# State-space turns written out with tables built ahead, a folded Fourier part, and late modulation columns on TensorE

## The reference

```
mod = c @ w_ada + b_ada                     # 6 vectors of 1024: sh_m, sc_m, gt_m, sh_f, sc_f, gt_f
h = rms_norm(x, g_pre_mix) * (1 + sc_m) + sh_m
u, f, q, k, v = split(h @ w_in)             # widths 384, 256, 384, 128, 128
y_ssm = s5_mixer(u, ...)                    # 24 groups of 16 channels, 64 complex states, both directions
y_fft = real(fft2(f over positions and over the 64 channels of a head)) @ w_fft
y_att = window_attention(q, k, v, sink)
x = x + gt_m * rms_norm(concat(y_ssm, y_fft, y_att) @ w_out, g_post_mix)
```

## Time and profile before

| | us |
|---|---|
| median of 3 runs | 3899.11 |
| lowest and highest | 3894.24, 3900.86 |
| the profiled execution | 3903.71 |
| its span, first to last instruction | 3901.9 |

### The profile page before, as it was taken

How to read it: one execution, slowest core, us unless ns; L and a number is a source line. 1 busy time by engine, 2 the same in 40 slices (tenths; PEclk the granted TensorE clock), 3 DMA queues, 4 the chain that set the end, 5 groups by cost and what they waited for, 6 DMA issues and landing times.

```text
span 3901.9 us, 41628 instructions
## 1 busy us (share of the span) xinstructions
PE 3400.1 (87%) x15935; PEld 2817.1 (72%) x15935; DVE 1191.4 (31%) x1793; ACT 790.4 (20%) x1395; POOL 1551.0 (40%) x1271
## 2 busy tenths in 40 slices
PE   6773334798999999999999999987788999999977
PEld 4663333687888878888888888876666888888866
DVE  4744664525233323210001123135534100001323
ACT  3020002513111112210000113136533100001222
POOL 3137663052333356523233573210025233336743
PEclk8887666999999999999999999989999999999999
DMA  4551001143111124311112333534433111122432
GB/s 170 152 181 44 7 7 38 45 157 130 44 54 43 54 103 140 97 54 43 54 43 82 118 118 122 166 116 107 108 108 108 44 54 43 54 81 99 149 108 92
DMA packets 261359, 344.97 MB, mean 88 GB/s; under 512 B 24726, under 2 KB 203209, under 8 KB 261234
## 3 DMA queue, kind: packets, MB, share of 16 engines
q1 hardware_dynamic: 217784, 258.76, 22.0%
q10 hardware_dynamic: 43098, 84.05, 5.9%
q0 software_dynamic: 352, 0.44, 0.0%
HBM read 293.50 MB, written 56.00 MB: 90 GB/s over the span
## 4 chain that ended last, share of the span: by engine, by line
PE 75%; DVE 11%; ACT 5%; issue 4%; DMA 2%; POOL 2%; SPq 0%; DVEq 0%; ACTq 0%; POOLq 0%
PE PS L811 67%; PE PS L1856 3%; DVE ot L1592 1%; PE PS L747 1%; DVE pl_ab L1964 1%; DVE pt L680 1%; PE PS L1544 1%; DMA w_raw<-w_up 1%; DVE oo L1593 1%; PE PS L1532 1%; ACT ph_ab L1901 1%; ACT act L702 1%; DVE t L1608 1%; ACT pr_ab L1891 1%; POOL w_lo L251 1%
## 5 line engine op out<-in xcount | busy, mean ns | idle before, releaser
L251 POOL TENSOR_TENSOR w_lo<-w_raw,w_hi 128x512 fp32r<-128x512 f32 x724 | 970.2, 1371 | 155.5 <-ACT w_hi L1303 130.9
L247 POOL CAST w_hi<-w_raw 128x2048 fp32r<-128x2048 f32 x173 | 335.7, 1941 | 1608.2 <-DMA w_raw<-ffn_w_gu 607.2
L811 PE MATMUL PS<-h_hi,w_hi 128*128 128x512 f32 x2482 | 803.6, 395 | 19.3 <-DVE h_lo L805 12.0
L811 PE MATMUL PS<-h_lo,w_hi 128*128 128x512 f32 x2482 | 796.6, 392 | 0.0
L811 PE MATMUL PS<-h_hi,w_lo 128*128 128x512 f32 x2482 | 796.0, 391 | 0.0
L811 PEld LDWEIGHTS PS<-h_hi,w_hi 128*128 128x128 f32 x2482 | 469.7, 189 | 120.0 <-DVE h_lo L805 16.6
L811 PEld LDWEIGHTS PS<-h_hi,w_lo 128*128 128x128 f32 x2482 | 469.8, 189 | 98.8
L811 PEld LDWEIGHTS PS<-h_lo,w_hi 128*128 128x128 f32 x2482 | 470.4, 190 | 95.7
L811 PE MATMUL PS<-w_hi,a_hi 128*128 128x512 f32 x1056 | 327.8, 392 | 9.5 <-DVE a_lo L877 7.2
L811 PE MATMUL PS<-w_lo,a_hi 128*128 128x512 f32 x1056 | 327.5, 392 | 0.0
L811 PE MATMUL PS<-w_hi,a_lo 128*128 128x512 f32 x1056 | 327.4, 391 | 0.0
...
## 6 DMA issues: line engine op xcount, KB each, us to landing
w_raw<-ffn_w_gu SPq DMA_DIRECT2D x88, 512.0 KB, 4.6
w_raw<-ffn_w_down SPq DMA_DIRECT2D x88, 512.0 KB, 4.2
w_raw<-w_up SPq DMA_DIRECT2D x44, 512.0 KB, 5.0
w_raw<-w_down SPq DMA_DIRECT2D x44, 512.0 KB, 4.2
xs<-px ACTq DMA_DIRECT2D x40, 512.0 KB, 2.6
w_raw<-w_out SPq DMA_DIRECT2D x32, 512.0 KB, 4.5
w_raw<-w_in SPq DMA_DIRECT2D x28, 512.0 KB, 5.1
...
```

Source lines behind the costliest of these rows:

```text
L247: e.tensor_copy(w_hi[b][:, 0:n], w_raw[b][:, 0:n]).then_inc(S("w_hi"), 1)
L251: op = e.tensor_tensor(w_lo[b][:, s], w_raw[b][:, s], w_hi[b][:, s].bitcast(F32), ALU.subtract)
L811: mm = e.matmul(o, a[ai], b[bi], start=start and first, stop=stop and end)
```

## The change

- `chain_dve` is cut in two: the exponential part (`chain_exp_dve`) runs in the start, ahead of the first modulation sums. The powers 2 to 8 are made by doubling, in 18 wider operations instead of 42. The exp on ScalarE and the head matrices of the Fourier part move to the start too.
- The four late modulation vectors leave VectorE and SP. GpSimd loads their 32 pieces into four buffers during the turns, and TensorE multiplies each with a column of c and adds all up in one PSUM bank. One sequence of gates follows behind the turns. The m slots go.
- u goes to DRAM from ScalarE and comes back in the order that the turns need, in 8 loads of SP. The t slots go.
- Fourier: since cosine is even and sine odd, f is folded (`fold_dve`) to 512 positions, the DFT table is 512 x 512 twice in 2 chunks, and output positions 513 to 1023 come from sums and differences (`fft_out_dve`). Position 512 is added by one-row matmuls with alternating signs. GpSimd makes both halves of the two chunks.
- Turns: written out one by one. All tables are made by VectorE. The rotations of all turns are cut into 16 x 8 factors (`rotations_dve`: copies and seven groups of four small operations), and `ssm_cs` multiplies them out per turn. `oo` has two buffers and is made one turn ahead, as is `gs_`. The sum `d_skip * u` becomes a 16 x 16 diagonal matmul. Outputs are formed channels first, so that GELU is done per turn, and go through DRAM (`yd`) into `yT`, instead of y_nat and the transposes.
- w_glu stage: VectorE multiplies with each sigmoid as soon as it is there.

The diff, cut to its core:

```diff
         G_Z1 = seg("z1", "cols", cols(t["w_in"]), 5)
-        G_DFT = seg("dft", "rows", rows(t["dft"]), 8)
+        G_DFT = seg("dft", "rows", rows(t["dft"]), 2)
...
-        def late_sp(e, first, end):
-            for i in range(first, end):
-                if i < 2:
-                    e.wait_ge(S("ht_lo"), 16)
-                else:
-                    e.wait_ge(S("lacc"), i - 1)
-                v, k = 2 + i // 8, i % 8
-                e.dma_start(lw[i % 2][:], t["w_ada"][0][k * P:(k + 1) * P, v * D:(v + 1) * D]).then_inc(S(f"lw_ld{i % 2}"), 16)
...
+        def ada_late_pe(e, first, end):
+            for q in range(first, end):
+                v, k = q // KT, q % KT
+                e.wait_ge(S(f"adl_ld{q % 4}"), 16 * (q // 4 + 1))
+                for h in range(2):
+                    r = 2 * v + h
+                    mm = e.matmul(PS[0:8, 0, :], cz[:, k, 7 - r:15 - r], adl[q % 4][:, h * 512:(h + 1) * 512],
+                                  start=q == 0 and h == 0, stop=q == 31 and h == 1)
+                mm.then_inc(S("ad_mm"), 1)
+        def ada_late_pool(e):
+            e.wait_ge(S("ff_y2"), 3)
+            for q in range(32):
+                v, k = q // KT + 2, q % KT
+                wait(e, S("ad_mm"), q - 3)
+                e.dma_start(adl[q % 4][:], t["w_ada"][0][k * P:(k + 1) * P, v * D:(v + 1) * D]).then_inc(S(f"adl_ld{q % 4}"), 16)
...
+            pr, pi = pw[:, PR:PR + CH + 1, :], pw[:, PI:PI + CH + 1, :]
+            for w in (1, 2, 4):
+                lo, hi = slice(1, w + 1), slice(w + 1, 2 * w + 1)
+                rw, iw = (v[:, w:w + 1, :].to_broadcast([2 * G, w, P]) for v in (pr, pi))
+                u, v = pwt[:, 0, 0:w, :], pwt[:, 1, 0:w, :]
+                tt(u, pr[:, lo, :], rw, ALU.mult)
+                tt(v, pi[:, lo, :], iw, ALU.mult)
+                tt(pr[:, hi, :], u, v, ALU.subtract)
+                tt(u, pr[:, lo, :], iw, ALU.mult)
+                tt(v, pi[:, lo, :], rw, ALU.mult)
+                tt(pi[:, hi, :], u, v, ALU.add)
+            e.wait_ge(S("sk_ld"), 32)
+            e.tensor_scalar(nsk[:], sk[:], -1.0, None, ALU.mult).then_inc(S("nsk"), 1)
             e.memset(junk[:, 0:1], 0.0).then_inc(S("pw"), 1)
...
         Z1 = [(0, "u", 0, P, 0, 0, 0), (0, "u", P, P, 0, 0, 1), (1, "u", 0, P, 0, 0, 2), (1, "f", P, P, 0, 0, 0),
-              (2, "f", 0, P, 0, 0, 1), (2, "q", P, P, 0, 0, 0), (3, "q", 0, P, 0, 0, 1), (3, "m", 0, P, 0, 0, 2),
-              (3, "q", P, P, 0, 0, 2), (4, "p", 0, P, 0, 0, 0), (4, "k", 0, P, 0, 0, 3), (4, "m", 0, P, 0, 0, 3),
-              (4, "p", 0, P, 0, 0, 1), (4, "t", 0, P, 0, 8, 0), (4, "t", 0, P, 0, 8, 1), (4, "v", P, P, 0, 8, 0),
-              (4, "t", 0, P, 0, 8, 2), (4, "m", 0, P, 0, 0, 4)]
-        u_tr = at("u_tr", [P, 3, SEQ], F32, 16 * KB)
+              (2, "f", 0, P, 0, 0, 1), (2, "q", P, P, 0, 0, 0), (3, "q", 0, P, 0, 0, 1), (4, "p", 0, P, 0, 0, 0),
+              (3, "q", P, P, 0, 0, 2), (4, "p", 0, P, 0, 0, 1), (4, "k", 0, P, 0, 0, 3), (4, "v", P, P, 0, 8, 0)]
+        u_tr = at("u_tr", [P, 3, CH, NCH], F32, 16 * KB)
...
+        def fold_dve(e):
+            e.memset(fm[:, :, 0:1], 0.0).then_inc(S("ff_fold"), 1)
+            e.wait_ge(S("z_uf"), 5)
+            e.tensor_tensor(fm[:, :, 1:512], fT[:, :, 1:512], fT[:, :, 1023:512:-1], ALU.subtract).then_inc(S("ff_fold"), 1)
+            e.tensor_tensor(fT[:, :, 1:512], fT[:, :, 1:512], fT[:, :, 1023:512:-1], ALU.add).then_inc(S("ff_fold"), 1)
...
-                    e.wait_ge(S("ff_lo"), T - 3)
-                for a in range(2):
-                    mm = e.matmul(PS[:, 4 + T % 4, a * 256:(a + 1) * 256], fT[:, a, T * P:(T + 1) * P],
-                                  bd[:, a, :, :].rearrange("p c n -> p (c n)"), start=True, stop=True)
-                mm.then_inc(S("ff_p"), 1)
-            e.wait_ge(S("ff_lo"), TT)
-            for kt in range(TT):
-                g = G_DFT + kt
+                mm = e.matmul(PS[0:1, 0, a * P:(a + 1) * P], fT[:, a, 512:513], bd[:, a, 0, :], start=True, stop=True)
+            mm.then_inc(S("ff_p"), 1)
+            e.wait_ge(S("ff_lo"), 5)
+            e.wait_ge(S("ff_hi"), 7)
+            for a in range(2):
+                cs = slice(a * P, (a + 1) * P)
+                for T in range(4):
+                    for q in (fp_hi, fp_lo):
+                        e.matmul(PS[:, 4, 2 * a:2 * a + 2], q[:, T, a, 0:P], altc[:], start=T == 0 and q is fp_hi, stop=False)
+                e.matmul(PS[:, 4, 2 * a:2 * a + 2], row_hi[:, cs], altr[:, 0:2], start=False, stop=False)
...
+        def fft_out_dve(e):
+            e.wait_ge(S("ff_os"), 1)
+            e.wait_ge(S("w_used"), G_DFT + 2)
+            e.tensor_tensor(yf[:, :, 0:512], PS[:, 0:2, :], os_[:], ALU.add).then_inc(S("ff_yf"), 1)
+            e.tensor_tensor(yf[:, :, 513:SEQ], PS[:, 0:2, 511:0:-1], os_[:, :, 511:0:-1], ALU.subtract).then_inc(S("ff_yf"), 1)
+            e.wait_ge(S("ff_y"), 1)
+            e.tensor_tensor(hl0[:, 3:5, :], yf[:, :, 0:512], hh[0][:, 3:5, :].bitcast(F32), ALU.subtract).then_inc(S("ff_y2"), 1)
...
+        def rotations_dve(e):
+            ta = own(e)
+            e.wait_ge(S("pw_ev"), 2)
...
+        def ssm_oo(e, ta, i):
...
+            g0 = i * GSUB
...
+            o = oo[i % 2]
+            for d in range(2):
+                qr, qi = (PR, PI) if d == 0 else (PRD, PID)
+                r, m = (st4(q, 9, d, g0).rearrange("p t g -> p g t").unsqueeze(3).to_broadcast([P, GSUB, 9, GC]) for q in (qr, qi))
+                c = [cc[:, k].rearrange("p (g c) -> p g c", c=GC)[:, g0:g0 + GSUB].unsqueeze(2).to_broadcast([P, GSUB, 9, GC])
+                     for k in range(2)]
+                for k in range(2):
+                    ta.add(e.tensor_tensor(o[:, k, d], r, c[k], ALU.mult))
+                if d:
+                    e.wait_ge(S("ss_oo"), 4 * i + 2)
+                for k in range(2):
+                    ta.add(e.tensor_tensor(oy[:, k], m, c[1 - k], ALU.mult))
+                ta.settle()
+                e.tensor_tensor(o[:, 0, d], o[:, 0, d], oy[:, 0], ALU.add).then_inc(S("ss_oo"), 1)
...
+        def ssm_cs(e, ta, i):
...
+            b = [turn_b[:, k, us].unsqueeze(2).to_broadcast([P, GB, 16, 8]) for k in range(2)]
+            for k in range(2):
+                ta.add(e.tensor_tensor(x[:, k], c, b[k], ALU.mult))
+            if i == 0:
+                e.wait_ge(S("ss_g"), 4)
...
+        def ssm_scan(e, ta, i):
+            g0 = i * GSUB
+            e.wait_ge(S("ss_g"), 4 * min(i + 2, TURNS))
+            e.wait_ge(S("ss_v"), i + 1)
...
+             .then_inc(S("ss_d"), 1)
+            e.wait_ge(S("ss_d"), i + 1)
+            ta.add(e.tensor_tensor(tY[:, 0], tY[:, 0], tY[:, 1], ALU.add))
+            ta.settle()
+            for u in range(GB):
+                r = u // GSUB * G + g0 + u % GSUB
+                rho = stn[:, RHO, r:r + 1].to_broadcast([P, NCH])
+                o, x = (tY[:, 1, u, :], tY[:, 0, u, :]) if u < GSUB else (tY[:, 1, u, ::-1], tY[:, 0, u, ::-1])
+                ta.add(e.tensor_tensor_scan(o, rho, x, 0.0, ALU.mult, ALU.add))
+            ta.settle()
+            wait(e, S("ss_y"), i)
+            n1 = NCH - 1
+            both = lambda v: v.unsqueeze(1).to_broadcast([P, 2, GSUB, n1])
+            e.tensor_tensor(av[:, :, 0, :, 1:], cs[:, :, 0:GSUB, 0:n1], both(tY[:, 1, 0:GSUB, 0:n1]), ALU.mult).then_inc(S("ss_av"), 1)
+            e.tensor_tensor(av[:, :, 1, :, 0:n1], cs[:, :, GSUB:GB, 1:], both(tY[:, 1, GSUB:GB, 1:]), ALU.mult).then_inc(S("ss_av"), 1)
...
+        def ssm_dve(e):
+            ta = own(e)
+            fft_lo_dve(e)
...
+            ssm_oo(e, ta, 0)
+            for par in range(2):
+                e.wait_ge(S(f"z_st{par}"), z_stores(0, par))
+            ssm_g(e, ta, 0)
+            fft_out_dve(e)
+            ssm_cs(e, ta, 0)
+            ta.add(e.memset(av[:], 0.0))
+            for i in range(TURNS):
+                if i + 1 < TURNS:
+                    ssm_oo(e, ta, i + 1)
+                    ssm_g(e, ta, i + 1)
+                ssm_scan(e, ta, i)
+                if i + 1 < TURNS:
+                    ssm_cs(e, ta, i + 1)
+            gates_dve(e)
+            for m in range(3):
...
+            def states(i):
+                g0 = i * GSUB
+                e.wait_ge(S("ss_g"), 4 * i + 4)
+                wait(e, S("ss_d"), i)
...
+                e.wait_ge(S(f"km{i % 2}"), 128 * (i // 2 + 1))
+                e.wait_ge(S("ss_av"), 2 * i + 2)
+                wait(e, S("ss_gl"), i)
                 for g in range(GSUB):
...
+            e.wait_ge(S("u_ld"), 128)
+            e.wait_ge(S("ss_dd"), 1)
+            e.wait_ge(S("ff_yf"), 2)
+            e.wait_ge(S("ff_os"), 1)
+            e.wait_ge(S("ff_5"), 1)
+            kernel_(0)
+            states(0)
+            for i in range(TURNS):
+                if i + 1 < TURNS:
+                    kernel_(i + 1)
+                    states(i + 1)
+                output(i)
+                ada_late_pe(e, ADA[i - 1] if i else 0, ADA[i])
```

(75 more changed lines are left out.)

682 lines of the change are left out of this document (303 added, 379 removed).

## The result

The changed kernel takes 3680.95 us (median of 4 runs, 3676.18 to 3686.49) where the kernel before takes 3899.99 beside it (3894.24 to 3905.28): ratio 0.9439, 95% interval 0.9420 to 0.9458. I had forecast 3710 with a range of 3690 to 3762; it is faster than the low end. The profiled execution has a span of 3678.1 us; the part behind the first softmax operation (the timetable's common point) lasts 3223.2 us where it lasted 3223.0. So the whole difference lies ahead of that point, which moved from 678.95 to 454.94, 224.0 us against the 189.5 of my sum.

The account below looks back on a forecast made before the run. It took the first 679 us as a relay that no engine fills, above all the state-space turns. First softmax moves from 678.95 to 489.4, 189.5 us less: 3903.7 becomes 3714, forecast 3710; own range 3692 to 3728, wider 3690 to 3762.

Parts of the forecast that it names:

- Turns: State-space loop: VectorE fills each turn, 38 us against 50.4 before, bounds 36.5 and 44; loop ends at 443.5.
- the tail: From output 5 to the softmax: output over at 450, GLU at 465.5, first softmax at 489.4 us.
- the ring: Turns: after a scan's PSUM read TensorE needs 15.6 to 19.6 us against VectorE's 16.2, a stall of 0 to 3.4.
- half hidden loads: Rival in the turns: late modulation chunks come every 5.1 us, 54 us a turn, total 3798; chance 0.06.
- Start and projection: Before the Fourier part: start net +1.5 us (bounds -1.5, +8), 22.8 us wait goes, projection ends at 192.6 instead of 224.4.
- Fourier: DFT falls from 192 to 48 matmuls, over by 220; VectorE's tables are late at 225, the loop starts at 243.
- Loads on GpSimd's queue: In the turns: 32 loads of 512 KB move from SP's queue, taken as 5 us each and covered by four buffers.
- a sign that the mechanism is wrong: TensorE waiting for `adl` loads, VectorE idle over 5 us a turn, or the softmax part over 5 us from 3223.
- the slower case (4040): Rival in the turns: late modulation loads hold TensorE at 12.8 us each, one behind the other, about 4040; chance 0.03.
- Low clock (3741): Rival in the turns: TensorE stays at the 1.2 GHz level and bounds the turn, 44.1 us, total 3741; chance 0.14.
- The part behind the softmax: From 679 us on nothing is edited, so its 3222.9 us were carried over unchanged.
- From the profiled execution to the median: Last step: the profiled execution lay 4.6 over the runs' median, so its 3714 became a forecast of 3710.

Follow-up runs that it names:

- Experiment 1: The changed kernel, but in its state-space part every VectorE operation waits for the one before it: 3701.12 us, turn 36.12 us.
- experiment 5: The changed kernel with the cs tables of turns 1 to 5 left out and turn 0's used again: 3668.85 us.
- experiment 2: The changed kernel, but each of a turn's eight scans waits for the one before it: 3682.55 us, turn 32.55 us.
- Experiment 7: Four kernels side by side: the changed kernel again (3678.29 us), GpSimd's w_out splits later (3670.50), late modulation chunks earlier (3675.95), both edits (3674.01).
- experiment 4: The changed kernel without 28 of the 32 late modulation chunks, their loads and matmuls left out: 3681.23 us.
- experiment 3: The changed kernel, but oo and g tables of the next turn are built behind the scan instead of ahead of it: 3717.14 us.

## Why the prediction was wrong, point by point

| point | before | forecast | measured |
|---|---|---|---|
| projection ends | 224.4 | 192.6 | 189.8 |
| Fourier result begins | | 225 | 219.3 |
| loop begins | | 243 | 241.3 |
| one turn | 50.4 | 38 | 31.57 |
| loop's last av ends | 633.3 | 443.5 | 407.7 |
| GLU matmuls begin | 653.5 | 465.5 | 429.3 |
| first softmax | 678.95 | 489.4 | 454.94 |

**The step that failed is "Turns".** Its mechanism was right: VectorE fills the turn, TensorE and the loads are covered, the clock rises. Its size was 6.43 us a turn too large, 32.2 in five turns, and 1.9 in the last scan part; the loop's start gives 1.7, the tail takes 1.3 back: 34.5, the whole difference between 489.4 and 454.94. Experiment 1 shows where 4.55 of the 6.43 are (its waits move the softmax by 26.8 us in all, 5.6 of them ahead of the first scan part): I had taken start-to-start durations of operations that each waited for the one before, for code whose diff replaces that wait by one per group. The new class `Tally` stood in the diff; I priced the operations and not the waits between them. The rest is 1 us for waits that those durations already held, and a stall of 0.9 that isn't there: 32 products that took 6.05 take 3.74 in the third turn, at this stage's granted clock, so the ring closes near 14.5 us (experiment 5) and not at 15.6 to 19.6. And my low bound of 36.5 came from rows of waiting operations alone. With 31.5 as bound the range would have begun 25 us lower and held the result. The scan row, besides, is from a turn of the register loop: the written-out turn of the same trace has 3.63 for the 4.40 (experiment 2).

Two sums beside it were loose. A turn of 36.5 to 41 and a start of -1.5 to +8 give 3700 to 3732 and not 3692 to 3728; and for half hidden loads 28 chunks at 5.1 us add 70 us in the loop and not 75.

**Start and projection: right.** First normalized half 2.2 us later (50.56 after, 48.37 before; forecast 1.5), the wait gone and nothing in its place, end 2.8 earlier than forecast.

**Fourier: end right (241.3 for 243), reason half wrong.** I had VectorE's tables late (225) and the DFT early (220). The DFT ended at 218.0, the tables, with the cheaper spacing, at 217.3, and VectorE waited 1.98 for TensorE; the first cs came 8.3 us behind the DFT's end, where I had named 10 or more. I had spread 7 us of GpSimd's contention over tables and result; it fell on the result and above all on the first cs, which took 13.0 instead of 7.1. Experiment 7 prices it at 8.1. So two errors cancel here: the tables were over 7.7 us before my time, and behind them came the wait of 1.98 and 4 us of contention more than I had allowed for the result and cs. That the loop began within 2 us of my time is luck.

**Loads on GpSimd's queue: right.** The view of DMA issues from 190 to 454 us gives 5.3 us to land (forecast 5):

```profile
adl<-w_ada POOLq DMA_DIRECT2D x24, 512.0 KB, 5.3
```

TensorE waited for these loads 4.7 us in all, at most 1.0 at a time. I had named such a wait as a sign that the mechanism is wrong, and the sign came; but the waits lie within TensorE's idle time, and experiment 4, without the loads of the turns, has the same turn. So neither the slower case (4040) nor the half hidden one (3798) came, and no delay of the loads by VectorE shows, which is busy 31.22 of 31.60 us beside them.

**Low clock (3741): did not come.** The granted clock is 0.88 in the turns. And experiment 4, with 0.68, has the same turn: with the six chunks the clock is higher, but with VectorE's tables one turn ahead nothing depends on it. Where they are not ahead (experiment 3) it costs some 1.2 us in every second turn.

**The part behind the softmax: right** (3223.2). **From the profiled execution to the median** I took off 4.6 us; the profiled one now lies 0.9 below its median, so this step made the miss smaller than the timetable's 34.5 and is itself no better than the spread of the runs.

## What to carry to other kernels

Price an operation by a row in which it stands between the same waits as in the new code: one that waits for its forerunner costs 0.12 us more from start to start here, a sixth of a 512-element product, and the displayed duration doesn't tell the two apart. Ask of every stage that gets faster which buffer it frees and which engine that starts: half a DFT less brought GpSimd's splits onto VectorE's tables and gained one us of two. Work on GpSimd is to be placed where VectorE waits anyway; the same splits cost 8 us in the Fourier result, 9.6 in a turn and next to nothing beside the GLU (12.2 us gained of the 12.8 that they and the moved chunks promise).

## What the chip showed beyond that

- Pairs of independent VectorE operations overlap by 0.08 us of their displayed durations (576 elements: 0.76 shown, 0.675 apart); scans by 0.07 (0.40 shown, 0.33 apart).
- Two 512-element operations beside a GpSimd split took 3.4 to 4.1 us instead of 1.29, so the loss is several times their own length, but over the whole overlap VectorE loses 0.4 to 0.6 of GpSimd's time (8.1 of 19.4, 9.6 of 17.2).
- The part behind the softmax, the same work in fourteen profiled executions, took 3214.0 to 3226.7 us: an edit worth less than some 6 us can be read in a stage and hardly in the total.
